# Main products that read and write their columns 16 at a time from two halves, with the input and the arena moved within 256 bytes

## What is computed

```python
# first block
z = rms_norm(h) @ w_in                      # 2048 -> 11264, split into heads and gates
y_a = chunkwise gated linear attention of z # 8 heads of 128
y_b = banded attention of z                 # 16 heads of 64
h = h + (gate_a * (y_a @ w_branch_a) + gate_b * (y_b @ w_branch_b)) @ w_out
h = h + square(relu(rms_norm(h) @ w_up)) @ w_down      # 2048 -> 8192 -> 2048
h = rms_norm(h)
# second block, with 16 meta tokens in front (272 tokens)
proj = rmsnorm(h) @ w_in_2                  # 2048 -> 6656
ya, yb = grouped-query attention with rope, differential attention
h = h + rmsnorm(concat(ya, yb) @ w_out_2)
```

## Time and profile before

| | |
|---|---|
| median of 3 runs | 1893.86 us (1893.37 to 1895.14) |
| span of the profiled execution | 1893.3 us |
| TensorE (PE) busy | 1879.6 us, 99% |
| TensorE weight loads (PEld) busy | 1743.7 us, 92% |
| DVE busy / ACT busy | 1101.4 us / 889.3 us |
| main products (L446 and L458) in the chain that ended last | 58% and 33% |
| granted TensorE clock | 0.999 of full speed |

### The profile page before, as it was taken

How to read it: one execution, slowest core, us unless ns; L and a number is a source line. 1 busy time by engine, 2 the same in 40 slices (tenths; PEclk the granted TensorE clock), 3 DMA queues, 4 the chain that set the end, 5 groups by cost and what they waited for, 6 DMA issues and landing times.

```text
span 1893.3 us, 33876 instructions
## 1 busy us (share of the span) xinstructions
PE 1879.6 (99%) x13432; PEld 1743.7 (92%) x13432; DVE 1101.4 (58%) x1270; ACT 889.3 (47%) x1171; POOL 143.6 (8%) x122
## 2 busy tenths in 40 slices
PE   9999999999999999999999999999999999999998
PEld 9989998999999889988998899899889999899986
DVE  6556766667655555545445445445565556767664
ACT  6544444455544445443444344334454355664543
POOL 2001322411001100000010000000010000000000
PEclk9999999999999999999999999999999999999999
DMA  8566565566565656656665665566556655354454
GB/s 270 184 181 177 181 179 178 165 200 180 168 231 191 214 186 179 194 198 192 196 192 193 194 191 194 194 190 190 189 185 181 179 170 150 105 147 144 156 190 143
DMA packets 176434, 346.47 MB, mean 183 GB/s; under 512 B 10976, under 2 KB 11184, under 8 KB 175776
## 3 DMA queue, kind: packets, MB, share of 16 engines
q1 hardware_dynamic: 174176, 337.76, 57.2%
q0 software_dynamic: 2128, 6.82, 1.4%
HBM read 342.44 MB, written 2.10 MB: 182 GB/s over the span
## 4 chain that ended last, share of the span: by engine, by line
PE 97%; DVE 1%; ACT 0%; DMA 0%; issue 0%; SPq 0%; DVEq 0%; ACTq 0%
PE ps L446 58%; PE ps L458 33%; PE ps L548 1%; PE ps L781 1%; DVE wlo L1301 1%; PE ps L771 1%; PE ps L748 1%; PE ps L791 0%; DMA raw<-in_w_in_dram 0%; ACT whi L899 0%; PE ps L476 0%; PE ps L759 0%; PE ps L599 0%; PE ps L591 0%; DVE xlo L1323 0%; PE ps L610 0%
## 5 line engine op out<-in xcount | busy, mean ns | idle before, releaser
L1301 DVE TENSOR_TENSOR wlo<-raw,whi 128x1024 fp32r<-128x1024 f32 x631 | 796.5, 1268 | 698.1 <-ACT whi L899 697.1
L899 ACT ACTIVATE whi<-raw 128x1024 fp32r<-128x1024 f32 x631 | 664.5, 1058 | 886.3 <-PE ps L446 551.5
L446 PE MATMUL ps<-xhi,whi 128*128 128x256 f32 (+1 forms) x1904 | 542.2, 285 | 0.4 <-DVE wlo L1301 0.3
L446 PE MATMUL ps<-xhi,wlo 128*128 128x256 f32 (+1 forms) x1904 | 531.3, 279 | 0.0
L446 PE MATMUL ps<-xlo,whi 128*128 128x256 f32 x1664 | 462.5, 278 | 0.0
L446 PEld LDWEIGHTS ps<-xhi,whi 128*128 128x128 f32 x1904 | 359.1, 189 | 9.3 <-issue 6.7
L446 PEld LDWEIGHTS ps<-xhi,wlo 128*128 128x128 f32 x1904 | 357.8, 188 | 0.0
L446 PEld LDWEIGHTS ps<-xlo,whi 128*128 128x128 f32 x1664 | 313.4, 188 | 1.5 <-issue 0.7
L446 PE MATMUL ps<-x2hi,whi 128*128 128x256 f32 x1024 | 282.8, 276 | 0.0
L446 PE MATMUL ps<-x2hi,wlo 128*128 128x256 f32 x1024 | 282.7, 276 | 0.0
L446 PE MATMUL ps<-x2lo,whi 128*128 128x256 f32 x1024 | 282.7, 276 | 0.0
(11 more groups left out here) (373 smaller groups left out, 2370.6 us busy)
## 6 DMA issues: line engine op xcount, KB each, us to landing
raw<-in_w_in_dram SPq DMA_DIRECT2D x279, 512.0 KB, 3.8
raw<-in_w_up_dram SPq DMA_DIRECT2D x128, 512.0 KB, 3.7
raw<-in_w_down_dram SPq DMA_DIRECT2D x128, 512.0 KB, 3.7
raw<-in_w_out_dram SPq DMA_DIRECT2D x64, 512.0 KB, 3.8
raw<-in_w_branch_a_dram SPq DMA_DIRECT2D x16, 512.0 KB, 4.9
raw<-in_w_branch_b_dram SPq DMA_DIRECT2D x16, 512.0 KB, 3.8
x_nat<-in_x_dram SPq DMA_DIRECT2D x4, 512.0 KB, 7.4
rel<-in_rel_turned_dram POOLq DMA_DIRECT2D x8, 256.0 KB, 4.3
```

Of the source, the lines that this page charges most:

```text
L446: ins = mm(outs[b], w[:, k % SLOTS, j, cols], v, start=start, stop=last and j == CK - 1 and i == 2, skip_group_check=True)
L899: f(whi[:, k % SLOTS], raw[:, k % SLOTS], ACT.Copy).then_inc(whi_ready, 1)
L1301: tt(wlo[:, k % SLOTS], raw[:, k % SLOTS], whi[:, k % SLOTS], ALU.subtract).then_inc(wlo_ready, 1)
```

## The change

The helper `woven` gives an access pattern over n columns that takes 16 from the first half, 16 from the second half, the next 16 from the first half, and so on (8 at a time where n is 272, which 32 does not divide). It is used on the moving operand and, with the same pattern, on the output in PSUM, so each column still lands in its place. The weight loads keep their pattern. The pad before `xhi` shrinks from 48 to 32 words, and the pad before `ident` is gone.

```diff
-X_PLACE = 48
-ARENA_PLACE = 16
+X_PLACE = 32
...
-        sb("arena_place", [P, ARENA_PLACE])
...
+        def woven(v, n):
+
+            run = 16 if n % 32 == 0 else 8
+            return spread(v, [run, n // 2 // run], [n // 2, 2], [1, run])
...
-                            ins = mm(outs[b], w[:, k % SLOTS, j, cols], v, start=start,
+                            ins = mm(woven(outs[b], n), w[:, k % SLOTS, j, cols], woven(v, n), start=start,
...
-                            ins = mm(ps[:, 2 * s + t, :], v[:, kt, toks], w[:, k % SLOTS, j, :],
+                            ins = mm(woven(ps[:, 2 * s + t, :], CW), v[:, kt, toks], woven(w[:, k % SLOTS, j, :], CW),
```

## The result

The changed kernel takes 1980.37 us (median of 4 runs, 1980.01 to 1980.57) against 1894.5 us before: ratio 1.0454, 95% interval 1.0439 to 1.0468. It is 86 us slower, where 84 us faster was forecast.

The account below looks back on a forecast made before the run. TensorE's cost per product was taken as the bound. A gain of 91.9 us, less 3 us of new waits and 5 for an imperfect lock, gave 84 us off 1893.3: 1809 on the span, 1810 forecast, range 1798 to 1897.

Parts of the forecast that it names:

- What bounds the kernel: TensorE is busy in 99% of the span at full clock, so only what one product costs TensorE can move the time.
- The price of the woven read: Jumps of the woven moving read in runs of 16 were taken to cost nothing.
- The other bound: Upper price of the woven read's jumps: 0.43 ns at each of 16, 6.9 ns a 256-column product, 13.8 of 512.
- The floor of 108.8 ns as what a single-pass product can reach: Main 256-column products could come down to the price that two-pass products show, about 2 ns beyond their column times.
- the 92 us of gain: Sum over all single-pass main products of their excess beyond the floor, 91.9 us if each comes down to it.
- The collision with the load: Moving read and weight load meeting in the same 64 bytes of 256 would explain the single-pass excess, 4.6 to 13.9 ns.
- The pads at nothing: New places, input 128 and arena 64 bytes off the rings, were costed at nothing, as L476 and L722 are clean.
- The long mode: The longer of two prices of 256-column products, 9.1 ns beyond the floor, counted for 1,464 products: 13.3 us.
- the write would decide: Price per jump of the output from which the PSUM write rival decides the outcome, given as 0.36 ns.
- The write to PSUM: Rival: the woven output pays one column time at each jump, 109 us against 92 gained, 1911 us; chance 0.11.
- The rival in step at the same place: In 5,760 products with arena operands, every read of the load meets one of the product: 1957 us; chance 0.08.
- The rival "one column time for every 64 bytes passed": Single-pass excess has nothing to do with the load; only the long mode could go, 1887 to 1894 us; chance 0.13.

Follow-up runs that it names:

- e2: Changed kernel (woven reads and writes) with the places of before, input and arena both 192 bytes after the rings: 1979.3 us, ratio 1.0441.
- e10: Woven reads and writes in runs of 16, places of before, each main-product weight load reading one word 128 times: 1978.9 us, ratio 1.045.
- e14: Kernel before, but the moving operand of 256- and 512-column products read in runs of 16, each run twice in a row: 1973.1 us, ratio 1.0411.
- e8: Reads and writes woven in runs of 64, 272 columns straight, places of before: 1895.5 us, ratio 1.000 to the kernel before.
- e13: Kernel before, but 256- and 512-column moving reads in runs of 16, every second one taken 256 bytes further on: 1894.0 us, ratio 0.9997.
- e7: Moving operand read in runs of 16 words, each beginning 12 words after the last began, output straight, places of before: 1913.4 us, ratio 1.0098.
- e12: Kernel before with straight reads and writes, input 224 and arena 0 bytes after the rings within 256: 1935.8 us, ratio 1.0224.
- fourth set: Four runs of the straight kernel before with other input and arena distances from the rings within 256 bytes: 1944.8, 1935.8, 1949.3 and 1912.2 us.
- e9: Kernel before, straight reads and its places, but each main-product weight load reads one word 128 times: 1916.3 us, ratio 1.012.
- e1: Kernel before with only the new places, input 128 and arena 64 bytes after the rings, reads and writes straight: 1943.3 us, ratio 1.0251.
- e4: Changed kernel with only the output written woven, moving operand read straight, places of the changed kernel: 1942.7 us, ratio 1.0248.
- e17: Main products reread the same 16 words as moving operand; each load reads one word 128 times, 64 bytes away: 2006.9 us, ratio 1.0596.
- e18: Moving operand rereads the same 16 words, each load one word 128 times, both at the same place within 256 bytes: 2001.8 us, ratio 1.0567.
- e5: Read woven, write straight, places of before, second partner of each pair of runs taken 128 bytes earlier: 2019.8 us, ratio 1.0663.
- e6: Reads and writes woven in runs of 32 in place of 16, 272 columns straight, places of before: 1953.5 us, ratio 1.0309.

## Why the prediction was wrong

**What bounds the kernel** was right: the profile after has the same busy share and clock and no new kind of wait, and the 86 us are in the distance between starts of the main products.

**The price of the woven read** is the step that failed. The prediction took nothing for it, because L548's runs of 32 cost nothing in two-pass products and "the run is nearer to 32 than to 1". But those products read at half the rate, and the single-pass ones do not behave like them. At the full rate, 32 columns on end at one place cost 36 column times (e2, e10, e14 and the changed kernel, all 120.0 and 240.0 ns), at load distances of 64, 128 and 192 bytes and with a load that reads a single word. The other bound, 0.43 ns a jump, would have put 256 columns at 108.8 + 6.9 = 115.7, 512 at 228.8; measured were 120.0 and 240.0, and the cost is not of the jump (e8, e13) but of the order of places (e14).

**The floor of 108.8 ns as what a single-pass product can reach** was taken from two-pass products too. No run reached it; the lowest measured in long pieces are 113.3 for 256 columns (before) and 226.7 for 512 (e7, e12). So the 92 us of gain was not shown to be there.

**The collision with the load.** An influence of the load exists: the straight read's time depends on its distance to the load (fourth set) and on what the load reads (e9). That it is a collision in the same 64 bytes is not shown, and the best distance for 512 columns, 0, speaks against it. The woven read does not part the two and win; it replaces a cost of 113.4 - 106.7 = 6.7 ns by one of 13.3 ns, the same at the three distances tried.

**The pads at nothing** was the second wrong term: alone they cost 47 us (e1). The rows used for it, two-pass products at 64 bytes with a clean 108.8, again said nothing of the full rate. In the changed kernel hardly any of this loss is left, since the woven read takes 120.0 at either pair of places; the two costs do not add.

**Two counts.** The long mode held some 1,728 products, not 1,464, and by the prediction's own counts the write would decide from 92 us over 260,000 jumps = 0.35 ns, not 0.36. Neither changes the forecast.

**The rivals.** The write to PSUM had the right sign and the wrong place: e4 shows that the woven write costs nothing, so for runs of 16 words (8 in the products of 272 columns) these runs contradict the sentence of the Trainium skill, SBUF — State Buffer, on cachelines, that any non-contiguous PSUM access slows matmuls. The rival in step at the same place had the right sign too, and e17 and e18 speak against its mechanism: reads held apart take 122.2 ns, reads held together 121.1 or 122.2. The rival "one column time for every 64 bytes passed" fitted 512 and 272 columns in the rows of before and did not survive the table: at distance 0 a product of 512 takes 226.7 and at 96 it takes 234.2, with as many bytes passed.

**What stays open.** Why staying at one place costs 2 column times in 18 is not shown. Nor is why the order 0, 2, 1, 3, 2, 0, 3, 1 of 64-byte places (e5) is slower still, 123.3 ns, though it never stays, why 192 bytes is the good distance, or what puts a stretch of products into one mode or the other. Loads of fewer words, which would show whether the cost of staying needs a load at all, were not run.

## What to carry to other kernels

A price read from instructions that run at half the rate did not hold at the full rate; where the trace has no row at that rate, keep both ends wide and forecast nothing from the floor. When moving operands and stationary operands are read side by side in single-pass fp32r products, as here, their distance within 256 bytes was worth up to 3% of this kernel's time, and is found by measuring a few pads. A measured good place belongs to one order of reading; a change that alters both needs one run with each part alone.

## What the runs showed of the hardware

- The time of a single-pass product depends on the order in which its moving read visits places within 256 bytes, and not on the jumps: for 256 columns 113.4 ns (117.8 in the long mode) with straight order at the jumps tried (e8, e13), 120.0 with each 64 bytes visited twice in a row (e2, e14), 118.8 with runs of 32 (e6), 121.1 or 122.2 where it never leaves 64 bytes (e17, e18), 123.3 in most pieces with the order of e5.
- A straight read's time depends on its distance to the stationary tile within 256 bytes, 113.4 to 120.0 ns for 256 columns and 226.7 to 234.2 for 512, with different best distances, and on what the weight load beside it reads (113.4 to 116.7 ns for the arena's products in e9).
- A write to PSUM in runs of 16 words from two halves of the output costs nothing: 1942.7 against 1943.3 us with a straight write (e4, e1).
